# Expert stage of a two-block model: a finished expert group leaves its accumulators ahead of two weight splits, its scatter stands one expert later, and the branch is taken ahead of the first gather

## The chip, the cores and the metric

The kernel runs on one core of one Trainium2 chip. The metric is the time of one execution on the device in microseconds, the median of several executions. The engines are TensorE (PE; its weight loads are shown as PEld), VectorE (DVE), ScalarE (ACT), GpSimd (POOL) and SyncE (SP, which here only issues weight loads).

## The reference, cut to what matters

The program is a first block (two feed-forward parts and a mixer) and a second block of two layers. Each layer of the second block mixes tokens and then runs a mixture of experts over 256 tokens of width 1024. The change touches the expert part alone:

```python
N_EXPERTS = 16; N_GROUPS = 4; EXPERTS_PER_GROUP = 4; TOP_K = 2; D_EXPERT = 256
scores = jax.nn.sigmoid((t @ router_w).astype(jnp.float32))
biased = scores + router_bias
grp_score = jnp.sum(lax.top_k(biased.reshape(T, 4, 4), TOP_K)[0], -1)
sel_group = jnp.argmax(grp_score, -1)             # one group of four experts per token
_, top_idx = lax.top_k(jnp.where(in_group, biased, -jnp.inf), TOP_K)
gates = ...                                       # two experts inside that group, normalised
h = jnp.einsum('td,edf->tef', t, w_gate_up)
a = jax.nn.silu(h[..., :D_EXPERT]) * h[..., D_EXPERT:] * gates[..., None]
y = jnp.einsum('tef,efd->td', a, w_down)
```

A token uses experts of one group only. So the four experts of a group work on the tokens of that group, at most 128 of them here, and their outputs can be added up before they go back to token order.

## The kernel before, in words

**Weights.** All weights are 32-bit and are used as a sum of two 16-bit parts. They come in units of 128 x 2048 values (1 MiB) through a ring of six slots (RING, line 33). SP loads a unit into `raw` (load, line 493) once the low part of the unit six before has been made. ScalarE makes the high part `whi` (hi_part, line 393; it waits for the load and for TensorE to have used the unit six before). VectorE makes the low part `wlo` (lo_part, line 402; it waits for the high part). These two instructions are a split. TensorE multiplies in three products, high x high, high x low and low x high (split_mm, line 621). An expert has three units, two of gate/up weights and one of down weights.

**The order of the work is written out by hand**, one list of instructions per engine, joined by semaphores. Each engine works through its own list in order. `emit(n)` on ScalarE (line 1547) and on VectorE (line 2070) stands for the next n splits of the ring.

**Ahead of the experts.** TensorE computes router logits and counts, for every token, its rank within its group (lines 1095 to 1099). VectorE's `ranks` (line 2034) copies the ranks and writes the largest group size into `rr[:, 18]`, with semaphore `rank_out`. VectorE's `places` (line 2040) then builds the selection matrices `p16`. TensorE's `gather(0)` (line 1101) multiplies the tokens with the matrix of group 0, so that its tokens stand in 128 slots. Now it is called ahead of the branch (lines 1112 to 1115). ScalarE and VectorE copy the result out as `ugh` and `ugl`. Each of the three engines then reads the largest group size into a register and branches (line 1267 on TensorE): over 128 tokens the dense way, otherwise the sparse way. The sparse way runs here, in both layers.

**Sparse way, TensorE (line 1242).** For each expert c of 16: `slots_in_half(c)` is the gate/up matmul of the group's slots, 96 matmuls of 128 columns in two halves, one for each weight unit. After experts 0 to 2 the gather of the next group follows. From c = 2 on `slots_down(c - 2)` follows, the down-projection, 12 matmuls of 512 columns. The down-projections of the four experts of a group add up in two PSUM banks, 6 and 7, the group's accumulators. `slots_down(4g)` opens them anew, so it waits until the earlier group has left them (`ys_lo`, line 1196). `scatter(g)` (line 1228, matmuls on line 1234) multiplies the group's 16-bit output with the transposed selection matrix, 8 matmuls of 512 columns, and adds it to the tokens' PSUM banks 0 to 3. It waits for `ys_lo` too. It stands after `slots_in_half` of c = 6, 10 and 14 for groups 0 to 2, and at the end for group 3.

**Sparse way, ScalarE (line 1590) and VectorE (line 2113).** For each expert ScalarE does the SiLU (line 1596), one split, the high part of the activations (line 1612) and two more splits. VectorE does the product (lines 2120 and 2126), one split, the low part of the activations (line 2131) and two more splits. At c = 5, 9 and 13 `group_out` follows these, for groups 0, 1 and 2: ScalarE copies the accumulators as `ysh` (line 1587, two instructions; it waits for the last down-projection of the group and, for the same buffer, for the scatter of two groups before). VectorE makes the rest `ysl` (line 2110, two instructions; `ys_lo`).

Of the kernel before, what the change touches and what calls it, by code (L numbers as in the profile page):

```python
# [37 lines left out]
EXPERTS = 16  # L38
# [121 lines left out]
def build(nc, a, out):  # L160
    small_d, b1_d, b2_d = a["const_small"], a["const_block1"], a["const_block2"]
    with ExitStack() as ctx:
# [457 lines left out]
        def _(pe):  # L620
# [325 lines left out]
            for l in range(LAYERS):  # L946
# [154 lines left out]
                def gather(g):  # L1101

                    for half in range(2):
                        for i, v in enumerate((xh, xl)):
                            for k in range(4 * half, 4 * half + 4):
                                o = ps[:, 2 * i + half, (k % 4) * P:(k % 4 + 1) * P]
                                for t in range(TT):
                                    last = pe.matmul(o, v[:, t, k * P:(k + 1) * P], p16[:, t, g * P:(g + 1) * P],  # L1108
                                                     start=t == 0, stop=t == 1)
                            last.then_inc(ga_mm[l], 1)  # L1110

                pe.wait_ge(xt_out, 4 * l + 4)
                pe.wait_ge(p_made0, 2 * l + 2)
                pe.wait_ge(rank_out, l + 1)
                gather(0)

                def gates():

# [13 lines left out]

                def dense():

                    pe.wait_ge(gates_made, l + 1)
                    gates()
                    pe.wait_ge(ga_hi[l], 2)
                    pe.wait_ge(ga_lo[l], 2)
                    residual()

                    def expert_down(c):
                        u = at_down(l, c)
                        pe.wait_ge(e_lo_made, EXPERTS * l + c + 1)
                        pe.wait_ge(lo_made, u.count(1))
                        hi, lo = ([v[:, c % 3, f * T:(f + 1) * T] for f in range(2)] for v in (d_hi, d_lo))
                        done = c == EXPERTS - 1
                        down(u, hi, lo, stop=done, done=True if done else None)

                    for c in range(EXPERTS):
                        if c >= 2:  # L1150
                            pe.wait_ge(e_m, EXPERTS * l + c - 1)
                        for half in range(2):
                            u = at_in(l, c) + half
                            pe.wait_ge(lo_made, u.count(1))
                            for kk in range(4):
                                k = 4 * half + kk
                                for col in range(4):
                                    w = slice(kk * HALF + col * P, kk * HALF + (col + 1) * P)
                                    last = split_mm(ps[:, 4 + 2 * (c % 2) + col // 2, (col % 2) * T:(col % 2 + 1) * T],
                                                    whi[:, u.slot, w], wlo[:, u.slot, w], uhi[:, k, :], ulo[:, k, :],  # L1160
                                                    k == 0 and col % 2 == 0, k == KT - 1)
                            last.then_inc(used, 1)
                        if c >= 2:
                            expert_down(c - 2)
                    expert_down(EXPERTS - 2)
                    expert_down(EXPERTS - 1)
                    pe.matmul(ps[0:32, 4, 0:1], zeros16[0:1, 0:32], zeros16[0:1, 0:1], start=True, stop=True,
                              skip_group_check=True).then_inc(used, 1)
# [71 lines left out]
                        last.then_inc(sc_mm2[l], 1)  # L1240

                def sparse():
                    for c in range(EXPERTS):
                        if c == 1:
                            pe.wait_ge(pT_out[l], 1)
                        slots_in_half(c)
                        if c == 0:
                            slot_setup()
                        if c < 3:
                            pe.wait_ge(ga_hi[l], 2 * c + 2)  # L1250
                            pe.wait_ge(ga_lo[l], 2 * c + 2)
                            gather(c + 1)
                        if c == 1:
                            pe.wait_ge(gbs_out[l], 4)
                        if c == 3:
                            pe.wait_ge(ga_hi[l], 8)
                            pe.wait_ge(ga_lo[l], 8)
                            residual()
                        if c in (6, 10, 14):
                            scatter(c // 4 - 1)  # L1260
                        if c >= 2:
                            slots_down(c - 2)
                    slots_down(EXPERTS - 2)
                    slots_down(EXPERTS - 1)
                    scatter(3)

                count = pe.value_load(rr[0:1, 18, 0:1].bitcast(I32))
                with pe.If(count > P):
                    dense()
# [7 lines left out]
        def _(act):  # L1277
# [130 lines left out]
            for i in range(10):  # L1408
# [14 lines left out]
                else:  # L1423
                    c = 256 * (i - 7)
# [27 lines left out]
            for l in range(LAYERS):  # L1452
# [137 lines left out]
                def sparse():  # L1590
                    emit(1)
                    for c in range(EXPERTS):
                        act.wait_ge(used, (at_in(l, c) + 1).count(1))
                        if c:
                            act.wait_ge(e_m, EXPERTS * l + c)
                        act.activation(e_act, ps[:, 4 + c % 2, 0:T], ACT.Silu, scale=1.0 / S).then_inc(e_silu, 1)
                        if c == 0:
                            act.wait_ge(pT_mm[l], 1)
                            act.activation(pT16.rearrange("p g n -> p (g n)"), ps[:, 5, :].bitcast(F16), ACT.Copy,
                                           scale=S / SX).then_inc(pT_out[l], 1)  # L1600
                            for g in range(4):
                                act.wait_ge(gbs_mm[l], g + 1)
                                act.activation(gbs[:, 4 * g:4 * g + 4, :],
                                               ps[:, 6 + g % 2, :].rearrange("p (k n) -> p k n", k=4),
                                               ACT.Copy).then_inc(gbs_out[l], 1)
                        if c < 3:
                            gather(c + 1)
                        emit(1)
                        act.wait_ge(e_made, EXPERTS * l + c + 1)
                        if c >= 3:  # L1610
                            act.wait_ge(used, at_down(l, c - 3).count(1))
                        act.activation(e_hi[:, c % 3, :], e_h, ACT.Copy).then_inc(e_hi_made, 1)
                        emit(2 if c < EXPERTS - 1 else 1)
                        if c in (5, 9, 13):
                            group_out(c // 4 - 1)
                    act.activation(flag[:, 5:6], zero8[:, 0:1], ACT.Sqrt)
                    group_out(3)

# [15 lines left out]
        def _(dve):  # L1634
# [286 lines left out]
            for l in range(LAYERS):  # L1921
# [191 lines left out]
                def sparse():  # L2113
                    emit(1)
                    for c in range(EXPERTS):
                        dve.wait_ge(e_silu, EXPERTS * l + c + 1)
                        if c:
                            dve.wait_ge(e_hi_made, EXPERTS * l + c)
                            dve.wait_ge(e_lo_made, EXPERTS * l + c)
                        dve.scalar_tensor_tensor(out=e_h, in0=ps[:, 4 + c % 2, T:2 * T], scalar=SX / S, in1=e_act,  # L2120
                                                 op0=ALU.mult, op1=ALU.mult).then_inc(e_m, 1)
                        if c == 0:
                            dve.wait_ge(gbs_out[l], 4)
                        dve.wait_ge(e_m, EXPERTS * l + c + 1)
                        hv = e_h.rearrange("p (k n) -> p k n", k=2)
                        dve.tensor_tensor(hv, hv, gbs[:, c, :].unsqueeze(1).to_broadcast([P, 2, P]), ALU.mult)                            .then_inc(e_made, 1)
                        if c < 3:
                            gather(c + 1)
                        emit(1)
                        dve.wait_ge(e_hi_made, EXPERTS * l + c + 1)  # L2130
                        dve.tensor_tensor(e_lo[:, c % 3, :], e_h, e_hi[:, c % 3, :], ALU.subtract).then_inc(e_lo_made, 1)
                        emit(2 if c < EXPERTS - 1 else 1)
                        if c in (5, 9, 13):
                            group_out(c // 4 - 1)
                    group_out(3)

                dve.wait_ge(gates_made, l + 1)
# [41 lines left out]
```

## Time and profile before

| | |
|---|---|
| median of 3 executions | 1338.1 us (1336.7 to 1341.34) |
| profiled execution, its own time | 1342.71 us |
| its span | 1340.9 us |
| mean granted clock of TensorE | 0.929 |
| TensorE matmuls busy | 1169.8 us, 87% |
| VectorE busy | 930.3 us, 69% |
| ScalarE busy | 667.9 us, 50% |
| expert stage of layer 0 | about 820 to 979 us of the span |
| expert stage of layer 1 | about 1167 to 1327 us of the span |

The span begins and ends with the profiled instructions; the execution's own time holds a little more. Lines such as L625 are helpers that many stages call, so their totals over the whole span say little about the expert stage. It has to be read in windows. The granted clock is the share of full speed that the chip gives to TensorE.

### The profile page before, as it was taken

Reading aid. Unit: us, or ns where it says so; the run is one execution under the profiler, and the core shown is the slowest. Engines: PE = TensorE matmul, PEld = TensorE weight load, DVE = VectorE, ACT = ScalarE, POOL = GpSimd, SP = SyncE. Lnnn points to the kernel's source line nnn. Section 1 sums busy time; section 2 is a strip of 40 time slices with the busy share of each in tenths; the row PEclk is TensorE's granted clock in tenths of the full one; section 3 lists DMA queues with packets and bytes.
Section 4 is the critical chain, followed back from the end, with each engine's and each line's share of the span. In section 5 each row is a group of like instructions: output and inputs, shape, how many; then the busy total and the mean of one; then the engine's idle time right before and its main releaser. Section 6 shows DMA issues by size and latency. Waiting matters only on the chain.

```text
span 1340.9 us, 24182 instructions
## 1 busy us (share of the span) xinstructions
PE 1169.8 (87%) x10316; PEld 900.0 (67%) x10316; DVE 930.3 (69%) x1145; ACT 667.9 (50%) x819; POOL 58.2 (4%) x75
## 2 busy tenths in 40 slices
PE   0499999799898899999897888999979978799995
PEld 0387777487786487776685548877668755697773
DVE  6689999465557555554548756998864775689985
ACT  1254433243345444442446546776653554577772
POOL 1001110150000000000100000000000000000000
PEclk9999999789798899999999797999989979699998
DMA  6999998423057365555544031999935303079970
GB/s 231 352 356 374 372 376 300 146 86 119 0 179 276 112 242 188 188 189 169 187 134 130 1 126 65 331 372 337 331 99 174 112 32 125 4 283 381 338 257 32
DMA packets 155451, 271.73 MB, mean 203 GB/s; under 512 B 9205, under 2 KB 95402, under 8 KB 155226
## 3 DMA queue, kind: packets, MB, share of 16 engines
q1 hardware_dynamic: 145946, 228.50, 49.4%
q0 software_dynamic: 6144, 32.41, 6.1%
q10 hardware_dynamic: 3264, 9.44, 2.1%
q8 instruction: 72, 1.18, 0.3%
q14 instruction: 25, 0.20, 0.0%
HBM read 269.28 MB, written 1.05 MB: 202 GB/s over the span
## 4 chain that ended last, share of the span: by engine, by line
PE 56%; DVE 28%; ACT 7%; issue 7%; DMA 1%; SPq 0%; DVEq 0%; ACTq 0%
PE ps L625 43%; DVE wlo L408 12%; DVE area L1728 6%; ACT whi L400 2%; PE ps L1234 1%; ACT area L1360 1%; DVE stat L1784 1%; DVE area L1778 1%; PE ps L826 1%; PE ps L815 1%; PE ps L872 1%; DMA area<-in_w_ada_dram 1%; PE ps L1108 1%; PE ps L705 1%; DVE hreg L1711 1%
## 5 line engine op out<-in xcount | busy, mean ns | idle before, releaser
L408 DVE SCALAR_TENSOR_TENSOR wlo<-raw,whi 128x2048 f16<-128x2048 f32 (+4 forms) x228 | 488.0, 2172 | 113.7 <-ACT whi L400 112.2
L400 ACT ACTIVATE whi<-raw 128x2048 f16<-128x2048 f32 (+4 forms) x228 | 403.3, 1805 | 34.8 <-PE ps L625 21.7
L625 PE MATMUL ps<-uhi,whi 128*128 128x256 f16 (+1 forms) x1200 | 326.1, 274 | 8.3 <-DVE ulo L1693 4.1
L625 PE MATMUL ps<-ulo,whi 128*128 128x256 f16 (+1 forms) x1200 | 326.0, 274 | 0.0
L625 PE MATMUL ps<-uhi,wlo 128*128 128x256 f16 (+1 forms) x1200 | 325.8, 273 | 0.0
L625 PE MATMUL ps<-whi,hreg 128*128 128x512 f16 x736 | 233.1, 387 | 5.4 <-DVE hreg L1716 5.4
L625 PE MATMUL ps<-area,whi 128*128 128x128 f16 (+2 forms) x2168 | 200.5, 225 | 8.6 <-issue 4.4
L625 PE MATMUL ps<-area,wlo 128*128 128x128 f16 (+2 forms) x1084 | 194.0, 225 | 0.0
L625 PEld LDWEIGHTS ps<-area,whi 128*128 128x128 f16 (+2 forms) x2168 | 175.1, 100 | 19.2 <-issue 8.2
L625 PE MATMUL ps<-wlo,hreg 128*128 128x512 f16 x368 | 142.5, 387 | 0.0
L625 PEld LDWEIGHTS ps<-uhi,whi 128*128 128x128 f16 x1200 | 119.3, 99 | 31.0 <-issue 8.8
L625 PEld LDWEIGHTS ps<-whi,hreg 128*128 128x128 f16 x736 | 73.5, 100 | 92.5 <-issue 8.3
L625 PEld LDWEIGHTS ps<-ulo,whi 128*128 128x128 f16 x1200 | 119.2, 99 | 17.4 <-issue 2.0
L625 PEld LDWEIGHTS ps<-uhi,wlo 128*128 128x128 f16 x1200 | 119.4, 99 | 13.9
L625 PEld LDWEIGHTS ps<-area,wlo 128*128 128x128 f16 (+2 forms) x1084 | 109.0, 101 | 0.0
L1728 DVE SCALAR_TENSOR_TENSOR area<-area,cond 128x768 f32 (+1 forms) x96 | 97.7, 1017 | 9.7 <-DMA area<-in_w_ada_dram 3.2
L1333 ACT ACTIVATE hreg<-ps 128x512 f32<-128x512 f32 x22 | 13.0, 593 | 103.9 <-PE ps L625 103.9
L625 PEld LDWEIGHTS ps<-wlo,hreg 128*128 128x128 f16 x368 | 36.7, 100 | 40.4 <-issue 4.2
L1335 ACT ACTIVATE hreg<-hreg 128x512 f16<-128x512 f32 x22 | 13.9, 630 | 88.3 <-DVE hreg L1711 88.3
L1711 DVE SCALAR_TENSOR_TENSOR hreg<-ps,hreg 128x512 f32<-128x512 f32 x22 | 15.1, 688 | 60.7 <-ACT hreg L1333 60.7
L1458 ACT ACTIVATE area<-ps 128x512 f32<-128x512 f32 (+4 forms) x32 | 17.4, 550 | 71.1 <-PE ps L625 60.5
L1360 ACT ACTIVATE area<-area,stat 128x128 f32<-128x128 f32 (+3 forms) x56 | 27.6, 493 | 39.0 <-DVE stat L1791 39.0
(300 smaller groups left out, 1383.5 us busy)
## 6 DMA issues: line engine op xcount, KB each, us to landing
raw<-in_exp_w_gate_up_dram SPq DMA_DIRECT2D x64, 1024.0 KB, 7.4
raw<-in_w_ffn_in_dram SPq DMA_DIRECT2D x44, 1024.0 KB, 7.4
raw<-in_w_in_dram SPq DMA_DIRECT2D x34, 1024.0 KB, 6.0
raw<-in_exp_w_down_dram SPq DMA_DIRECT2D x32, 1024.0 KB, 8.0
area<-in_w_ada_dram POOLq DMA_DIRECT2D x36, 768.0 KB, 7.7
raw<-in_w_ffn_out_dram SPq DMA_DIRECT2D x22, 1024.0 KB, 7.3
raw<-in_w_out_dram SPq DMA_DIRECT2D x12, 1024.0 KB, 5.8
area<-in_w_ada_dram ACTq DMA_DIRECT2D x12, 768.0 KB, 6.0
```

What stands on the lines that cost most here:

```text
L400: act.activation(whi[:, u.slot, 0:n], raw[:, u.slot, 0:n], ACT.Copy, scale=SW).then_inc(hi_made, 1)
L408: dve.scalar_tensor_tensor(out=wlo[:, u.slot, 0:n], in0=raw[:, u.slot, 0:n], scalar=SW, in1=whi[:, u.slot, 0:n], op0=ALU.mult, op1=ALU.sub ...
L625: last = pe.matmul(o, st, mv, start=start and i == 0, stop=stop and i == 2, skip_group_check=True)
L705: last = pe.transpose(ps[:, 4 + k // 2, (k % 2) * T + t * P:(k % 2) * T + (t + 1) * P], xn[:, t, k * P:(k + 1) * P], ident)
L815: pe.matmul(ps[:, n % 3, 128:384], q[:, 128:256], k, start=True, stop=True).then_inc(sc_mm, 1)
L826: last = pe.transpose(ps[:, 3 + n % 3, c * P:(c + 1) * P], src[:, c * P:(c + 1) * P], ident)
L872: last = pe.matmul(ps[:, 4, 8 * j + c:8 * j + c + 1], acc[:, m * D + c * P:m * D + (c + 1) * P], ones[:, 0:1], start=True, stop=True)
L1335: act.activation(hhi[:, par, :], h_f32, ACT.Copy).then_inc(h_hi, 1)
L1360: last = act.activation(s_, s_, ACT.Exp, bias=st[:, 2 + t:3 + t], accum_out=st[:, 4 + t:5 + t])
L1458: act.activation(dst, src, func, scale=1.0 / S).then_inc(proj_out, 1)
L1711: dve.scalar_tensor_tensor(out=h_f32, in0=ps[:, 5 + 2 * par, :], scalar=SX / S, in1=s_act, op0=ALU.mult, op1=ALU.mult).then_inc(h_made, 1)
L1728: dve.scalar_tensor_tensor(out=v, in0=aring[:, k // 2, k % 2, :], scalar=cond[:, k:k + 1], in1=v, op0=ALU.mult, op1=ALU.add).then_inc(ada_ ...
```

## The change

Three edits, in both layers. On ScalarE and VectorE `group_out` of groups 0 to 2 stands ahead of the expert's last two splits instead of behind them. On TensorE the scatter of groups 0 to 2 stands after the gate/up matmuls of experts 7, 11 and 15 instead of 6, 10 and 14. And TensorE's wait for the largest group size, the register load and the branch stand ahead of the first gather, which is now the first thing in either way.

```diff
--- before.py
+++ after.py
@@ tensor
-                pe.wait_ge(xt_out, 4 * l + 4)
-                pe.wait_ge(p_made0, 2 * l + 2)
-                pe.wait_ge(rank_out, l + 1)
-                gather(0)
+                def first_gather():
+
+                    pe.wait_ge(xt_out, 4 * l + 4)
+                    pe.wait_ge(p_made0, 2 * l + 2)
+                    gather(0)
...
                 def dense():
 
+                    first_gather()
                     pe.wait_ge(gates_made, l + 1)
...
                 def sparse():
+                    first_gather()
                     for c in range(EXPERTS):
...
-                        if c in (6, 10, 14):
+                        if c in (7, 11, 15):
                             scatter(c // 4 - 1)
                         if c >= 2:
                             slots_down(c - 2)
...
+                pe.wait_ge(rank_out, l + 1)
                 count = pe.value_load(rr[0:1, 18, 0:1].bitcast(I32))
                 with pe.If(count > P):
                     dense()
@@ scalar
                         act.activation(e_hi[:, c % 3, :], e_h, ACT.Copy).then_inc(e_hi_made, 1)
-                        emit(2 if c < EXPERTS - 1 else 1)
                         if c in (5, 9, 13):
                             group_out(c // 4 - 1)
+                        emit(2 if c < EXPERTS - 1 else 1)
@@ vector
                         dve.tensor_tensor(e_lo[:, c % 3, :], e_h, e_hi[:, c % 3, :], ALU.subtract).then_inc(e_lo_made, 1)
-                        emit(2 if c < EXPERTS - 1 else 1)
                         if c in (5, 9, 13):
                             group_out(c // 4 - 1)
+                        emit(2 if c < EXPERTS - 1 else 1)
```

## Rows read from the trace of the kernel before

**Rows 1.** The page, busy us, share of the span, instructions, TensorE.
```profile
PE 1169.8 (87%) x10316; PEld 900.0 (67%) x10316; DVE 930.3 (69%) x1145; ACT 667.9 (50%) x819; POOL 58.2 (4%) x75
```

**Rows 2.** Chain of waits, 880 to 925 us: start, us, what.
```profile
884.10 0.69 DVE area L2110
...
884.85 1.90 PE ps L1234 x8
```

**Rows 3.** Timeline of TensorE, experts 5 and 6: start, us, instruction [idle before].
```profile
869.37 0.28 PE L625 MATMUL ps<-area,whi 128*128 128x128 f16 x2
...
874.73 0.38 PE L625 MATMUL ps<-whi,hreg 128*128 128x512 f16 x1
...
877.32 0.28 PE L625 MATMUL ps<-area,whi 128*128 128x128 f16 x2
...
884.85 1.90 PE L1234 MATMUL ps<-area 128*128 128x512 f16 x8 [2.00 <-DVE area L2110]
...
886.58 0.38 PE L625 MATMUL ps<-whi,hreg 128*128 128x512 f16 x1
...
889.17 0.28 PE L625 MATMUL ps<-area,whi 128*128 128x128 f16 x2
```

**Rows 4.** Timeline of TensorE, second stop of layer 0, last of layer 1.
```profile
913.02 0.28 PE L625 MATMUL ps<-area,whi 128*128 128x128 f16 x2
...
920.54 3.06 PE L1234 MATMUL ps<-area 128*128 128x512 f16 x8 [1.99 <-DVE area L2110]
...
926.55 0.28 PE L625 MATMUL ps<-area,whi 128*128 128x128 f16 x2
...
1297.97 0.28 PE L625 MATMUL ps<-area,whi 128*128 128x128 f16 x2
...
1311.49 0.28 PE L625 MATMUL ps<-area,whi 128*128 128x128 f16 x2
```

**Rows 5.** Windows: stretch, length, busy by engine, granted clock, DMA share, GB/s.
```profile
820.00:824.00 4.00, 3.78 (x36) 3.81 (x37) 3.59 (x14) 1.11 (x1) 0.00 (x0) 0.50 0.02 4
...
876.00:884.00 8.00, 6.84 (x103) 5.93 (x101) 7.97 (x7) 7.22 (x8) 0.00 (x0) 1.00 1.04 393
...
916.00:924.00 8.00, 6.01 (x56) 3.71 (x54) 7.96 (x8) 6.02 (x7) 0.00 (x0) 0.82 1.04 398
```

**Rows 6.** Timeline of VectorE, step of expert 5 and accumulators of group 0.
```profile
876.37 0.41 DVE L2120 SCALAR_TENSOR_TENSOR hreg<-ps,hreg 128x256 f32<-128x256 f32 x1
...
879.70 4.49 DVE L408 SCALAR_TENSOR_TENSOR wlo<-raw,whi 128x2048 f16<-128x2048 f32 x2
884.10 1.28 DVE L2110 SCALAR_TENSOR_TENSOR area<-ps,area 128x512 f16<-128x512 f32 x2
```

**Rows 7.** Timeline of ScalarE, the same stretch.
```profile
877.60 3.69 ACT L400 ACTIVATE whi<-raw 128x2048 f16<-128x2048 f32 x2
881.20 1.06 ACT L1587 ACTIVATE area<-ps 128x512 f16<-128x512 f32 x2
```

**Rows 8.** Timeline of SP, landing of that load, ScalarE's split of it.
```profile
884.21 0.37 SPq L498 DMA_DIRECT2D raw<-in_exp_w_down_dram  x1
...
DMA to landing us min/median/max: 9.9/9.9/9.9
...
898.92 1.90 ACT L400 ACTIVATE whi<-raw 128x2048 f16<-128x2048 f32 x1
```

**Rows 9.** Timeline around the branch, VectorE's count, then TensorE in both layers.
```profile
813.80 0.15 DVE L2038 CAST area<-area 128x1 int32<-128x1 f32 x1
...
814.70 1.55 PE L1108 MATMUL ps<-area 128*128 128x128 f16 x18 [1.42 <-DVE area L2042]
...
820.22 0.37 PE L625 MATMUL ps<-area,whi 128*128 128x128 f16 x2 [2.48 <-issue]
...
828.10 0.61 PE L1211 MATMUL ps<-diag,area 128*128 128x128 f16 x8
...
1167.14 0.37 PE L625 MATMUL ps<-area,whi 128*128 128x128 f16 x2 [1.91 <-issue]
...
1173.98 0.22 PE L1211 MATMUL ps<-diag,area 128*128 128x128 f16 x1
```

## The prediction

> **What bounds the kernel now.** I read the page first: TensorE is busy for 87% of the span, so in most stages it sets the pace and what counts is where it stands still [rows 1]. Then the chain of waits through the expert stage of layer 0. It goes back from a scatter (line 1234) to VectorE's accumulator step (line 2110) [rows 2]. So I took the timeline of TensorE alone. From the start of expert 0 to the end of the last down-projection, its stops of more than half a microsecond all lie ahead of scatter(0), scatter(1) and scatter(2). One expert costs 5.36 us for its gate/up matmuls (869.37 to 874.73) and 2.59 us for a down-projection (874.73 to 877.32), 7.95 us together [rows 3]. Gate/up of expert 6 starts at 877.32 and is through at 882.68 by that count, but scatter(0) starts at 884.85 with 2.00 us of idle time put down to line 2110. The scatter itself takes 1.73 us at full clock (884.85 to 886.58) and the down-projection after it 2.59.
>
> The cost of a stop is best read from the start of one gate/up to the start of the next. First stop: 877.32 to 889.17 is 11.85 us, where 5.36 + 1.73 + 2.59 = 9.68 would do. 2.17 us are lost [rows 3]. The other five lose more: 913.02 to 926.55 is 13.53 and 1297.97 to 1311.49 is 13.52, so 3.85 each [rows 4]. The extra 1.68 us is the clock: the eight matmuls of scatter(1) span 3.06 us against 1.90 in scatter(0), and the granted clock of the 8 us around the stop is 0.82 against 1.00 for the eight around the first. Between stops the clock is 1.00 [rows 4, 5]. Total in the six stops: 2.17 + 5 x 3.85 = 21.4 us.
>
> **Accumulators ahead of two splits.** Per group two ScalarE copies and two VectorE subtractions move ahead of two splits on each engine; nothing is added and the move holds no DMA. On VectorE, expert 5 begins at 876.37, its low half is done where the two splits begin, at 879.70, and the accumulator step follows them at 884.10, 1.28 us long by the row and 1.20 us in pitch [rows 6]. ScalarE's copies stand at 881.20 behind two splits from 877.60, 1.06 us [rows 7]. In the new order ScalarE copies from about 877.6 to 878.7. What it waits for, the end of down-projection 3, is there at 877.32 [rows 3]. VectorE then works from 879.70 to about 880.9 instead of 884.1 to 885.3, 4.4 us earlier. TensorE wants the result at 882.68, where down-projection 4 re-uses those banks. It is ready with some 1.7 us to spare, so the wait doesn't reappear there. Here ScalarE comes to them 2.9 us after gate/up 5 ends, and the down-projection takes 2.59; where ScalarE is less behind it may wait some tenths, which the 1.7 us hold.
>
> **What is queued behind.** The two splits that now follow are 1.2 us later on VectorE. TensorE needs the earlier of them (second half of expert 7) at 885.27 + 2.68 = 887.95; it is done at 883.1. The other (down weights of expert 5) is done at 885.3 and read at 892.4. Next expert's step starts at 885.3 as before. SP loads a ring slot only after the split of the unit six before, so two loads per group go out 1.2 us later. The tightest one was issued at 884.21, took 9.9 us to land (894.1), and ScalarE split it at 898.92, 4.8 us later [rows 8]. With TensorE's stop gone ScalarE comes 2.2 us sooner, and with the load 1.2 us later about 1.4 us is left. If that is used up ScalarE stalls, but TensorE reads this unit only some 8 us after the split, so the first microseconds cost nothing.
>
> **Scatter one expert later.** Eight matmuls per group stand behind gate/up 7, 11, 15 instead of 6, 10, 14; their input is then 8 us old. The same number of matmuls, at full clock 1.73 us, no cost. The buffer of group g is next written by group g+2, eight experts on, so no new wait. At 15 it also gives expert 15's low half 1.7 us more cover ahead of its down-projection.
>
> **Is VectorE next?** It needs 7.73 us per expert (876.37 to 884.10) against TensorE's 7.95, and per group 4 x 7.73 + 1.2 = 32.1 against 4 x 7.95 + 1.73 = 33.5 [rows 3, 6]. It stays 1.4 us per group inside. Followed expert by expert with these durations, the distance between the two only grows in VectorE's favour after group 0, and the last group's tail is as before. So all 21.4 us should go. Bounds: 0 if every wait comes back at the down-projection, 21.4 if none does. I take 21.4, since the spare time of 1.7 us is from rows.
>
> **The branch ahead of the first gather.** Now the gather starts at 814.70, behind VectorE's first selection matrices, and expert 0 at 820.22 with 2.48 us idle put down to issue; in layer 1 it is 1.91 us [rows 9]. That is value_load and branch. The count is out at 813.95 (813.80 + 0.15). Behind a wait on it the branch would let the gather start at 813.95 + 1.9 to 2.5 = 815.9 to 816.5, some 1.5 us later than now, and expert 0 follows the gather at once: its inputs for the first half were copied a microsecond before. Net -1.0 us in layer 0, -0.4 in layer 1. Then the clock. Expert 0 ran at half (0.50 from 820 to 824) and took 7.88 us up to 828.10; in layer 1 it took 6.84, where 5.36 would do: 2.5 and 1.5 us lost [rows 5, 9]. Gather and expert 0 become one unbroken run of 7.2 us at full clock, and what was a second slow start between them falls away; the first remains. I count half of the 4.0 us. Layer 0 and 1 together: -1.4 - 2.0 = -3.4, taken as 3. Bounds: -6 if the whole slow start goes, +2 if the branch takes 2.5 us longer in its new place, with the gather's own instructions behind it. VectorE's gate chain shifts later by some 1.5 us with the gather, and is still through before expert 0 ends; slot_setup does not wait long.
> The row shows only that the branch costs 1.91 to 2.48 us behind a gather. The Trainium skill (Runtime: NRT & Kernel Launch, "Instruction fetch mechanics") says that prefetch is sequential and that a taken branch out of the window stops the sequencer for a fetch. By that rule the move hides none of the stall except the 0.75 us in which TensorE waits for VectorE anyway, and both layers would give 1.5 us of idle time and what the clock gives beside it; no row here shows a fetch.
>
> **Sum.** Against the profiled execution's own 1342.7 us (span 1340.9, 1.8 around it): -21.4 - 3 = 1318.3. That execution is 4.6 us over the median of 1338.1; I take the difference, 24.4, off the median: **1314 us**, -1.8%.
>
> **Rivals.**
> A. The wait comes back ahead of down-projection 4g, one expert earlier than the scatter it left. VectorE would have to be over 1.7 us later against TensorE than the rows have it, for which the saturated VectorE of experts 4 to 6 speaks (busy 7.97 of 8 us [rows 5]), and its 1.4 us of slack per group against. With 1 us of waiting and the clock's 1.68 in all six: 21.4 - 16 = 5.4 saved, and 3 from the branch: 1330.
> B. Weights become the bound. A group's 12 loads of 1.05 MB in 33.5 us are 375 GB/s. The DMA share is already 1.04 with 393 GB/s in the stretch before the first stop and loads took up to 9.9 us there [rows 5, 8]. For it: landing times rise while VectorE asks for three loads per 7.73 us. Against: 393 is above 375, and no engine waits for a weight load in this stage now. If the rate stayed at what the stage moves now per group (12.6 MB in 37.4 us, 337 GB/s), 3.85 us of each of 4 groups would be lost again, less some 8 us that the ring is ahead: about 7.4 per layer, 15 in all, time 1329.
> The Trainium skill (DMA: Bandwidth & Descriptors, "Where 436 GB/s comes from") gives about 358 GB/s per core for loads from HBM. The 393 of the trace is over that. As an estimate by the page, a group would take 35.1 us in place of 33.5; the 6.4 us in four groups are within the ring's 8, or cost up to 3 us in both layers, 1317.
> C. The move is one for one: accumulators can't leave earlier, since ScalarE's copies wait for down-projection 4g+3, and TensorE stops as long at the new place. Against: that projection ends at 877.32, ScalarE started the copies 3.9 us later [rows 3, 7]. Time 1336 to 1338.
> D. Slower. VectorE falls behind at the down-projection as in A, but by 3 us: each stop then costs 3 + 1.68 = 4.7, six of them 28 against the 21.4 removed: 1338.1 + 6.7 - 3 = 1342. It decides from the point where VectorE is 5.6 us later against TensorE than now (1.7 spare + 3.85 paid today), which a lost 0.6 us per expert would bring about by the third group.
>
> **Chances.** Forecast 0.78, A 0.07, B 0.07, C 0.05, D 0.03. Nine tenths lie between 1309 (branch bound of -6, executions a little under the median) and 1331; with a tenth to each side left out I give 1309 to 1328. Faster by over 0.3% (4 us, about what a measurement of this kernel tells from no change): 0.92, within 0.3%: 0.05, slower: 0.03.
>
> **What would show it.** Right: no idle time on TensorE ahead of any scatter but the last of a layer; 9.68 us from gate/up 7 to gate/up 8; granted clock 1.00 from expert 1 to 15; line 2110 about 4.4 us earlier against expert 5's step; gather at 816 and expert 0 directly behind it. Wrong: idle time put down to line 2110 ahead of a down-projection (A, C, D); ScalarE's line 400 waiting for a DMA of expert weights (B); a gather later than 817.

## The result and the profile after

| | before | changed |
|---|---|---|
| median | 1339.13 us (1336.7 to 1341.34, 4 runs) | 1319.53 us (1317.37 to 1321.82, 4 runs) |
| profiled execution, own time | 1342.71 us | 1319.91 us |
| its span | 1340.9 us | 1318.1 us |
| mean granted clock | 0.929 | 0.939 |

The ratio is 0.9852, with a 95% interval of 0.9831 to 0.9874: 19.6 us faster by the medians, 22.8 us by the two profiled executions. Beside it on another chip the changed kernel came to 0.9819 (0.98 to 0.9839), 23.1 us (experiment 5). The forecast was 24.4 us less.

**The stops are gone.** TensorE's timeline of the changed kernel around the first scatter, lines that answer to [rows 3]: start, us, instruction, and in brackets idle time where there is any.

```profile
877.26 0.28 PE L625 MATMUL ps<-area,whi 128*128 128x128 f16 x2
...
882.62 0.38 PE L625 MATMUL ps<-whi,hreg 128*128 128x512 f16 x1
...
885.21 0.28 PE L625 MATMUL ps<-area,whi 128*128 128x128 f16 x2
...
890.57 1.89 PE L1236 MATMUL ps<-area 128*128 128x512 f16 x8
...
892.29 0.38 PE L625 MATMUL ps<-whi,hreg 128*128 128x512 f16 x1
...
894.88 0.28 PE L625 MATMUL ps<-area,whi 128*128 128x128 f16 x2
```

Gate/up 6 ends and down-projection 4 starts at 882.62 with no bracket behind it. From gate/up 7 (885.21) to gate/up 8 (894.88) it is 9.67 us, 9.68 by the forecast's count. The other five places read the same: from scatter to scatter it is 33.52 or 33.53 us in both layers. In the chain of waits of the changed kernel the groups follow each other as matmuls alone: start, us, what.

```profile
858.93 31.80 PE ps L625 x432
890.73 1.73 PE ps L1236 x8
892.46 31.80 PE ps L625 x432
924.26 1.73 PE ps L1236 x8
925.98 31.80 PE ps L625 x432
957.78 1.73 PE ps L1236 x8
```

31.80 + 1.73 = 33.53 us per group, the count of the forecast, where the kernel before took 35.7 or 37.4.

**Why TensorE finds the result ready.** VectorE's timeline of the changed kernel, the step of expert 5; it answers to [rows 6]. The accumulators leave at 879.63, directly behind the low half of expert 5's activations, and the splits follow from 880.83. TensorE wants the first bank at 882.62. Both halves of the result are there 1.7 to 1.8 us earlier; the forecast had 1.7. The true spare time is longer. Each half has a wait of its own in the down-projection (line 1196 of the kernel before), the first half is done 0.68 us after the start, at 880.31, and only this half is wanted at 882.62. That is 2.3 us.

```profile
879.29 0.42 DVE L2135 TENSOR_TENSOR hreg<-hreg 128x256 f16<-128x256 f32 x1
879.63 1.28 DVE L2114 SCALAR_TENSOR_TENSOR area<-ps,area 128x512 f16<-128x512 f32 x2
880.83 4.48 DVE L408 SCALAR_TENSOR_TENSOR wlo<-raw,whi 128x2048 f16<-128x2048 f32 x2
```

**Clock and weights.** A window of 100 us in the changed kernel's expert stage, columns as in [rows 5], and all waits that the profile lists from 850 to 960 us: who waited for whom, total us, times, longest.

```profile
850.00:950.00 100.00, 100.00 (x1355) 81.97 (x1353) 97.33 (x80) 75.77 (x66) 0.00 (x0) 1.00 1.03 379
```

```profile
ACT hreg L1600 <- PE ps L625: 15.5, 12, 2.6
ACT hreg L1616 <- DVE hreg L2130: 10.4, 9, 2.8
DVE wlo L408 <- ACT whi L400: 1.8, 2, 0.9
```

TensorE is busy for all of 100 us, the clock is full, VectorE is at 97%, the weights arrive at 379 GB/s, and nobody waits for a load.

**The branch.** Here the profile differs from the forecast. TensorE's timeline of the changed kernel, the lines that answer to [rows 9]:

```profile
818.97 3.25 PE L1108 MATMUL ps<-area 128*128 128x128 f16 x29 [4.81 <-issue]
822.34 0.42 PE L625 MATMUL ps<-area,whi 128*128 128x128 f16 x2
828.04 0.61 PE L1213 MATMUL ps<-diag,area 128*128 128x128 f16 x8
...
1153.50 3.89 PE L1108 MATMUL ps<-area 128*128 128x128 f16 x32 [4.82 <-issue]
1157.19 0.42 PE L625 MATMUL ps<-area,whi 128*128 128x128 f16 x2
1162.72 0.61 PE L1213 MATMUL ps<-diag,area 128*128 128x128 f16 x8
```

The idle time ahead of expert 0 is gone, but 4.81 us stand ahead of the gather where 1.42 stood. The view of the branch's own line gives the cause: the compare-and-branch in TensorE's queue, of the kernel before (line 1268) and of the changed one (line 1272). The three numbers are the shortest, median and longest in ns.

```profile
L1268 PEldq COMPARE_BRANCH  x2: 3466/3670/3873, 816.2 to 1163.5; - x2
```

```profile
L1272 PEldq COMPARE_BRANCH  x2: 3358/3454/3551, 815.4 to 1149.8; - x2
```

It lasts about as long in both places. Before, it began at 816.2, while the array still worked on the gather up to 817.7: the queue had taken in all of the gather, and 1.5 us of the branch were hidden under it (1.7 in layer 1). Ahead of the gather the array has nothing left to do.

ScalarE and VectorE take the same way in the same kernel, over their own dense ways, and their branches cost next to nothing. The same view for the kernel before, lines 1621 and 2139:

```profile
L1621 ACTq COMPARE_BRANCH  x2: 45/50/54, 817.5 to 1164.8; - x2
...
L2139 DVEq COMPARE_BRANCH  x2: 63/65/67, 823.4 to 1170.7; - x2
```

So taking the branch is not enough to make it dear. TensorE's dense way has 96 gate/up matmuls for each of 16 experts, and those of the other two have only a few instructions and three splits for each.

### The profile page after: what moved, and what is told of

Same layout as the page of the kernel before. It is cut to its first block, busy times and chain, and to the rows that moved or that the text cites. A ratio compares the mean times of both kernels' runs of the same rounds, so it can differ in the third digit from the quotient of the medians.

```text
span 1318.1 us, 24182 instructions
## 1 busy us (share of the span) xinstructions
PE 1157.3 (88%) x10316; PEld 894.2 (68%) x10316; DVE 929.4 (71%) x1145; ACT 667.6 (51%) x819; POOL 58.2 (4%) x75
## 4 chain that ended last, share of the span: by engine, by line
PE 66%; DVE 21%; ACT 6%; issue 5%; DMA 1%; SPq 0%; DVEq 0%; ACTq 0%
PE ps L625 53%; DVE wlo L408 6%; DVE area L1732 6%; PE ps L1108 1%; ACT area L1364 1%; ACT whi L400 1%; DVE stat L1788 1%; DVE area L1782 1%; PE ps L1236 1%; PE ps L729 1%; PE ps L826 1%; PE ps L815 1%; PE ps L872 1%; PE ps L705 1%; DMA area<-in_w_ada_dram 1%
## 5 line engine op out<-in xcount | busy, mean ns | idle before, releaser
L625 PE MATMUL ps<-whi,hreg 128*128 128x512 f16 x736 | 229.6, 382 | 5.4 <-DVE hreg L1720 5.4
L625 PE MATMUL ps<-area,whi 128*128 128x128 f16 (+2 forms) x2168 | 196.7, 223 | 4.2 <-DVE area L1967 4.2
L625 PE MATMUL ps<-area,wlo 128*128 128x128 f16 (+2 forms) x1084 | 190.3, 223 | 0.0
```

The lines of the kernel that those rows point to most:

```text
L625: last = pe.matmul(o, st, mv, start=start and i == 0, stop=stop and i == 2, skip_group_check=True)
```

## The experiments

Experiments 1 to 4 ran on one chip, 5 to 8 on a second and 9 and 10 on a third, each time beside the kernel before; times and ratios are against it. Only the lines that an edit changes are printed, against the changed kernel unless said otherwise; three dots stand for code left out.

### 1. Groups only: the branch stays behind the first gather

```diff
-                def first_gather():
-
-                    pe.wait_ge(xt_out, 4 * l + 4)
-                    pe.wait_ge(p_made0, 2 * l + 2)
-                    gather(0)
+                pe.wait_ge(xt_out, 4 * l + 4)
+                pe.wait_ge(p_made0, 2 * l + 2)
+                pe.wait_ge(rank_out, l + 1)
+                gather(0)
...              (first_gather() goes out of both ways)
-                pe.wait_ge(rank_out, l + 1)
                 count = pe.value_load(rr[0:1, 18, 0:1].bitcast(I32))
```

> Accumulators ahead of the splits and scatter one expert later; the branch stays behind the first gather. Theory 1 (the gain is the six stops, 2.17 + 5 x 3.85 = 21.4 us, and the moved branch is worth next to nothing: its idle time grew from 2.48 + 1.42 to 4.81 us in layer 0 while the slow start got shorter): 21 us under the kernel before, within 1 to 2 us of the changed kernel, idle ahead of expert 0 again about 2.5 and 1.9 us. Rival 1 (the branch carries the forecast's 3 us): 18 us under before. Rival 2 (the moved branch costs, since its compare-and-branch of 3.4 us stands alone ahead of the gather): this kernel is 1 to 3 us faster than the changed one.

1317.77 us against 1342.22: 0.9825 (0.9801 to 0.9849), 24.4 us faster. No stop ahead of scatters 0 to 2 in either layer, idle time ahead of expert 0 back at 2.26 and 2.02 us. From the first router matmul to the end of expert 0 its profile has 19.84 and 18.22 us, 38.06 together, where the changed kernel has 38.18. So the forecast's 24.4 us are reached without the moved branch; against the changed kernel's 0.9852 and 0.9819 no difference can be told.

### 2. Branch only

```diff
-                        if c in (7, 11, 15):
+                        if c in (6, 10, 14):
...              (ScalarE and VectorE)
-                        if c in (5, 9, 13):
-                            group_out(c // 4 - 1)
                         emit(2 if c < EXPERTS - 1 else 1)
+                        if c in (5, 9, 13):
+                            group_out(c // 4 - 1)
```

Against the kernel before, only the branch has moved.

> Only the branch stands ahead of the first gather; accumulators and scatter as before. Theory 1: within 2 us of the kernel before, idle time ahead of the gather 4.8 us in both layers, none ahead of expert 0, and the six stops stay at 2.0 us of idle each. Rival 1: 3 us faster. Rival 2: 1 to 3 us slower.

1335.12 us against 1342.22: 0.995 (0.9935 to 0.9964), 7.1 us faster, more than any theory had. Idle time ahead of the gather is 4.79 us in both layers and none stands ahead of expert 0. Most of the gain is not at the branch. From the first router matmul to the end of expert 0 this kernel takes 18.99 and 19.45 us, against 19.97 and 20.01 before: 1.5 us. Most of the rest seems to stand in the stops, which this profile has all six, each with 2.0 us idle. TensorE's timeline of this kernel, second and third stop of layer 0:

```profile
917.18 1.90 PE L1236 MATMUL ps<-area 128*128 128x512 f16 x8 [1.99 <-DVE area L2114]
...
952.88 3.56 PE L1236 MATMUL ps<-area 128*128 128x512 f16 x8 [2.00 <-DVE area L2114]
```

The same 2.0 us of idle time once leave the scatter at 1.90 us and once at 3.56. Measured from gate/up to gate/up, a stop costs 2.17 us or 3.84, hardly anything between: here four times the small price and twice the large, 16.4 us, in the profile before once and five times, 21.4 us. This goes beyond one profile: the mean granted clock is 0.936 to 0.942 in the 12 executions of this kernel, and 0.929 to 0.935 in the 23 of the kernel before beside them. On the other two chips the kernel before reached 0.937 and 0.939, though. The reading is that with the moved branch fewer of the stops lower the clock, and that this gain falls away once there are no stops. It fits the runs but is not shown: one profile of each kernel was kept, and these two also differ by 2.4 us ahead of the router and by 1.4 us, the other way, between the layers, where the kernels are the same. What decides whether a stop of 2 us lowers the clock stays open.

### 3. Accumulators only: the scatter stays at 6, 10, 14

```diff
-                        if c in (7, 11, 15):
+                        if c in (6, 10, 14):
                             scatter(c // 4 - 1)
```

The branch stays behind the gather as in experiment 1, so against the kernel before only `group_out` has moved.

> Only the accumulators leave ahead of the two splits; the scatter stays at experts 6, 10 and 14, the branch as before. Theory 1 (the stop was the late low half, and that is 1.7 us early at the old scatter too): no stop ahead of a scatter, same time as with the later scatter within 1 us, 21 us under before. Rival 3 (both moves are needed, since the scatter takes the result as soon as it is there): stops of 0.3 us or more ahead of the scatters and 3 us or more slower than with both.

1317.31 us, 0.9828 (0.9802 to 0.9854), 24.9 us faster: the same as with the later scatter. Its scatter(0), at the old place, has no bracket:

```profile
879.07 1.89 PE L1234 MATMUL ps<-area 128*128 128x512 f16 x8
```

The whole gain that can be measured is in the accumulators' place. The second edit adds nothing to it.

### 4. Scatter only

The edit is against the kernel before.

```diff
-                        if c in (6, 10, 14):
+                        if c in (7, 11, 15):
                             scatter(c // 4 - 1)
```

> Only the scatter stands one expert later; the accumulators leave behind the splits as before. Theory 1 (down-projection 4g re-uses the banks, so it waits for the same low half): the stop moves one for one from the scatter to down-projection 4, 8, 12, about 2.0 us of idle each, clock at half behind it in most; time of the kernel before within 2 us. Rival 4 (the later scatter is what removes the stop): 15 to 21 us faster.

1338.54 us, 0.9979 (0.9965 to 0.9993), 3.7 us faster, where at most 2 were expected. TensorE's timeline of this kernel shows the stop of group 0 at down-projection 4 instead of the scatter:

```profile
883.70 0.38 PE L625 MATMUL ps<-whi,hreg 128*128 128x512 f16 x1 [2.10 <-DVE area L2110]
```

All six are there, moved one for one, twice at 2.25 us and four times at 3.92, 20.2 us together. This is rival C of the prediction, true of the scatter's move alone. The 3.7 us are not explained; the stops' prices in the two profiles differ by 1.2.

### 5. The changed kernel again, beside three other branches

> The changed kernel once more, on one chip beside the next three. Theory 1: 19 to 23 us under before. It is the base of the comparison with the other branch orders.

1316.83 us against 1339.97: 0.9819 (0.98 to 0.9839), 23.1 us faster. The next three ran beside it.

### 6. The sparse way directly behind the compare, branch behind the gather

The gather stands as in experiment 1. On top of that:

```diff
-                with pe.If(count > P):
-                    dense()
+                with pe.If(count <= P):
+                    sparse()
                 with pe.Else():
-                    sparse()
+                    dense()
```

> Groups as in the change, the branch behind the first gather as before, and on TensorE the condition turned round, so that the way that is taken stands directly behind the compare and the dense way behind it. The trace has compare-and-branch at 3.4 to 3.9 us. Theory 5 (the sequencer waits for instructions from a far place; The Trainium skill, Runtime: NRT & Kernel Launch, 'Instruction fetch mechanics', says a taken branch out of the window has to fetch): compare under 0.5 us, no idle time ahead of expert 0, 2.3 and 2.0 us of idle less and less of the slow start, 4 to 8 us faster than with the branch as before. A jump of 3.5 us over the dense way then stands behind the last scatter of layer 0, half hidden by the 2.8 us in which TensorE waits there. Rival 5 (the compare itself costs 3.5 us whichever way it goes): no difference.

1311.8 us, 0.9781 (0.9761 to 0.9801): 5.0 us under the changed kernel, from which it differs in two edits. From experiment 1 it differs in this one alone; that ran on another chip, and 0.9781 against 0.9825 is 5.9 us. No idle time between gather and expert 0. Theory 5 holds, and rival 5 does not. Behind the last scatter of layer 0 TensorE stands for 3.54 us instead of 2.83, so the jump over the dense way shows there with 0.7 us. TensorE's timeline of this kernel, at that place:

```profile
969.66 1.83 PE L715 MATMUL ps<-small,xn 128*128 128x128 f32 x8 [3.54 <-DVE xn L1676]
```

### 7. The same with the branch ahead of the gather

The turned condition of experiment 6 on the changed kernel; nothing else differs.

> The changed kernel with the condition turned round on TensorE. Theory 5: idle time ahead of the gather back from 4.8 to about 1.4 us, none ahead of expert 0, the same time as the last one within 1 us or up to 1 us faster. Rival 5: 4.8 us stay, same time as the changed kernel.

1310.56 us, 0.9775 (0.9755 to 0.9795): 29.4 us under the kernel before and 6.3 under the changed kernel, the cleanest comparison, with one edit on one chip. From experiment 6 it can't be told. The line of the branch, the whole kernel and then layer 0's compare alone:

```profile
L1272 PEldq COMPARE_BRANCH  x4: 80/1956/4420, 810.4 to 1294.0; - x4
...
L1272 PEldq COMPARE_BRANCH  x1: 80/80/80, 810.4 to 810.4; - x1
```

And TensorE's timeline, at the gather, where VectorE's selection matrices end the idle time again, and behind the last scatter of layer 0, where the idle time is 3.44 us against the changed kernel's 2.83:

```profile
810.61 3.14 PE L1108 MATMUL ps<-area 128*128 128x128 f16 x32 [1.52 <-DVE area L2046]
...
819.38 0.61 PE L1213 MATMUL ps<-diag,area 128*128 128x128 f16 x8
...
964.51 1.82 PE L715 MATMUL ps<-small,xn 128*128 128x128 f32 x8 [3.44 <-DVE xn L1680]
```

The same instruction takes 80 ns when it falls through; in the kernels with the dense way first it is taken to a place behind that way and takes 3.3 to 3.9 us. The two long ones of the four are now jumps at the end of the layers (4.42 and 3.83 us). The Trainium skill (Runtime: NRT & Kernel Launch, "Instruction fetch mechanics") says that prefetch is sequential and that a taken branch out of the window has to fetch first. These runs agree, with 0.08 against 3.5 us on TensorE and 0.05 to 0.07 us for the taken branches of ScalarE and VectorE over their much shorter dense ways. No run has a near target on TensorE.

### 8. No branch on TensorE

```diff
-                count = pe.value_load(rr[0:1, 18, 0:1].bitcast(I32))
-                with pe.If(count > P):
-                    dense()
-                with pe.Else():
-                    sparse()
+                sparse()
```

It leaves out TensorE's dense way, which these inputs don't take.

> Groups as in the change; TensorE has no register load, no compare and no dense way (it always goes the sparse way, which is what these inputs ask for); ScalarE and VectorE branch as before. It measures all that TensorE's branch costs: Theory 5 and Rival 5 both expect no idle time ahead of expert 0 and 4 to 8 us under the kernel with groups only; if the kernel with the sparse way first is within 1 us of it, nothing of the branch is left to gain.

1310.21 us, 0.9777 (0.9752 to 0.9801). Its interval is 3.3 us to each side, and it can't be told from experiments 6 and 7. Of what the branch costs on TensorE, turning the condition round gets back all that can be measured. In the profile TensorE stands for 2.83 us behind the last scatter of layer 0 here, so 0.6 to 0.7 us of the jump are left in those two.

### 9. Accumulators between the two splits

```diff
                         if c in (5, 9, 13):
+                            emit(1)
                             group_out(c // 4 - 1)
-                        emit(2 if c < EXPERTS - 1 else 1)
+                            emit(1)
+                        else:
+                            emit(2 if c < EXPERTS - 1 else 1)
```

> The changed kernel with the accumulators leaving between the two splits, one ahead and one behind, on both engines. It tests the 1.7 us of spare time at down-projection 4g: VectorE's low half comes one split (2.2 us) later, its first part at about 882.5 and its second at 883.1 in group 0, against a need at 882.7 and 884.0. Theory 1: stops of 0 to 0.5 us ahead of down-projections 4, 8, 12 that don't lower the clock, time within 2 us of the changed kernel. Rival A of the prediction (VectorE is so late that the wait comes back): stops of 1.5 us or more and 5 us or more over the changed kernel.

1316.83 us against 1339.88: 0.9833 (0.9805 to 0.9862), 23.1 us faster, as much as the changed kernel in experiment 5. No bracket ahead of down-projections 4, 8 and 12 or scatters 0 to 2; from scatter(0) at 887.86 to scatter(1) at 921.43 it is 33.57 us, 0.04 more than in the changed kernel. VectorE's accumulators and TensorE's down-projection 4 in this kernel:

```profile
879.09 1.28 DVE L2117 SCALAR_TENSOR_TENSOR area<-ps,area 128x512 f16<-128x512 f32 x2
...
879.92 0.38 PE L625 MATMUL ps<-whi,hreg 128*128 128x512 f16 x1
```

The accumulators are 2.2 us later, more than the 1.7 us of the prediction, and still nothing stops: the first half is out at 879.77, 0.15 us ahead of the down-projection. This fits a spare time of 2.3 us. One split behind the accumulators is enough, and rival A's wait does not arise even with nearly all of the spare time used up.

### 10. ScalarE's copies behind the splits, VectorE's part ahead

```diff
 # ScalarE only
+                        emit(2 if c < EXPERTS - 1 else 1)
                         if c in (5, 9, 13):
                             group_out(c // 4 - 1)
-                        emit(2 if c < EXPERTS - 1 else 1)
```

> The changed kernel with ScalarE's copies behind its two splits as before, VectorE's part ahead of its splits. VectorE then stands at its wait for the copies (from 879.6 to about 881.9 in group 0) with both splits queued behind it. Theory 1: the low half is there at 883.2, TensorE stops 0.1 to 0.3 us at down-projection 4, VectorE loses 2 us per group, of which its slack per group takes 1.4; stops grow a little in groups 1 and 2, time 0 to 4 us over the changed kernel. Rival 6 (ScalarE's order doesn't matter): no difference and no idle time on VectorE.

1321.96 us, 0.9868 (0.9841 to 0.9895), 5.1 us over experiment 9 beside it, a little more than expected. VectorE now stands for the copies with its splits queued behind them. TensorE does not stop in group 0, and stops for 0.5 us in groups 1 and 2. In layer 0 it stops once more ahead of the last down-projection, for expert 15's activations, which no theory had. VectorE's and TensorE's timeline of this kernel, in layer 0:

```profile
879.07 1.29 DVE L2114 SCALAR_TENSOR_TENSOR area<-ps,area 128x512 f16<-128x512 f32 x2 [2.03 <-ACT area L1591]
...
914.16 0.38 PE L625 MATMUL ps<-whi,hreg 128*128 128x512 f16 x1 [0.52 <-DVE area L2114]
...
948.40 0.38 PE L625 MATMUL ps<-whi,hreg 128*128 128x512 f16 x1 [0.56 <-DVE area L2114]
...
964.37 0.39 PE L625 MATMUL ps<-whi,hreg 128*128 128x512 f16 x1 [0.95 <-DVE hreg L2135]
```

From scatter to scatter the four stops of 0.5 us cost 0.7 us each, and the scatter behind them spans 1.89 us: stops this short don't lower the clock here. The last one costs 1.1 us. That is 3.9 of the 5.1 us. So VectorE's part alone brings most of the gain, 17.9 of some 23 us, and ScalarE's part the rest.

## Why the prediction was right, and where it was off

- **Where the time stood.** Right. Six stops, 21.4 us, all gone. Experiment 1 has this, with the later scatter, at 24.4 us (20.3 to 26.7 by its interval), and 3 and 4 show that the accumulators' place does it.
- **The wait does not come back at down-projection 4g.** Right, and with more to spare than was worked out: 1.7 us count from the end of both halves, but at 882.6 only the first is wanted, so it is 2.3. Experiment 9 used up a split of 2.2 us of it and lost nothing. Rivals A and D did not occur.
- **Scatter later at no cost.** Right; at no gain either (3 against 1).
- **VectorE stays inside, the supply holds.** Right. A group takes 33.53 us as counted. Rival B does not occur: 379 GB/s over 100 us is above the 375 asked for, where the kernel before moved 357 in the same window. The Trainium skill's 358 GB/s for loads from HBM (DMA: Bandwidth & Descriptors, "Where 436 GB/s comes from") is passed here; the measurement decides.
- **The two later loads.** The load that had 9.9 us in [rows 8] was issued at 885.3 in the changed kernel and landed 8.5 us later. No engine waited for one.
- **The branch.** The direction of its total was right and its terms were not. The forecast had the gather start 1.5 us later than before and 1.4 us less idle time over both layers. Measured from the count (814.70 + 0.15) the gather starts 4.1 us later instead of 1.9 to 2.5. In layer 0 the idle time grew from 1.42 + 2.48 to 4.81 us, in layer 1 from 1.42 + 1.91 to 4.82, 2.4 us in all. The step that failed is "that is value_load and branch": the 1.91 to 2.48 us of idle time were taken for the whole cost of the branch, and they were only what stuck out from under the gather. The branch's own line, 3.47 to 3.87 us in the kernel before, was there to be read; the register load ahead of it is 0.3 to 0.5 us more. The estimate that the prediction set beside the fetch rule, 1.5 us of idle time gained in both layers, fails on the same step: it took it that before none of the stall was hidden, and 1.5 to 1.7 us of it were in each layer. The clock gave more than the half that was counted: expert 0 took 5.70 and 5.53 us against 7.88 and 6.84, 3.5 us where 2.0 were taken. The stage from the first router matmul to the end of expert 0 went from 19.97 and 20.01 to 19.01 and 19.17 us: 1.8 us gained, of 3.4 worked out, of which 3 went into the sum. Even of these 1.8, 1.1 stand in layer 1 between the first router matmul and the last rank matmul, ahead of the branch in both kernels (6.27 against 5.13 us); experiments 1, 3 and 4, with the branch in its old place, have 5.23 to 5.27 there. And experiment 1 takes no longer over the whole stage than the changed kernel. A gain by the moved branch, beside the accumulators, is not shown.
- **The sum.** 21.4 + 1.8 = 23.2, and the profiled executions differ by 22.8: 23.7 from the first router matmul of layer 0 on, and 0.9 the other way ahead of it, where the kernels are the same (that matmul stands between 804 and 809 us in all profiles). The medians of the first measurement differ by 19.6 (16.9 to 22.6 by the interval), those in experiment 5 by 23.1. The time came out 5.5 us over the forecast. 1.0 of this is the kernel before, whose median is 1339.13 here and was taken at 1338.1, and 1.2 is the branch, 1.8 in place of 3. The other 3.6 no row explains: 23.2 lies just above the interval of the first measurement and inside that of experiment 5 (21.6 to 26.8). One cause was not tested: the 21.4 us were read from one execution, which took longer than the other three known by then, and in which five of six stops were dear. Experiments 2 and 4 have two and four dear ones, and with fewer of them there is less to save.
- The prediction named a gather later than 817 as a sign that its branch step was wrong. It came at 818.97. The signs for the accumulators were all met: no idle time ahead of scatters 0 to 2, 9.67 us from gate/up to gate/up, a granted clock of 1.00 from expert 1 on, and the accumulators 4.4 us earlier against expert 5's step.

## What to carry to other kernels

When an engine that bounds the time stands still at a point, look in the queue of the engine that it waits for at what stands ahead of the awaited instruction, and let the awaited work go first if the work behind it has slack. Price such a stop from start to start of the repeating work, clock included, and expect it to be worth more or less when its place shifts. Put the way that is taken directly behind the compare, and don't take idle time behind a branch for its cost: look at the branch's own line in the queue.

## What the runs showed of the hardware

- A compare-and-branch on TensorE took 0.08 us when it fell through and 3.3 to 3.9 us when it was taken over the dense way; 1.5 to 1.7 us of this were hidden while the array worked through matmuls issued ahead of it. ScalarE's and VectorE's, taken over their short dense ways, took 0.05 to 0.07 us.
- The same stop of 2.0 us cost either 2.17 or 3.85 us. Stops of 0.5 us cost 0.7 (experiment 10).
- With 3.4 us more idle time ahead of the gather, and the stops as before, the mean granted clock was 0.936 to 0.942 against 0.929 to 0.935 on the same chip, and the time 7.1 us less, of which 1.5 stood at the moved place (experiment 2). Why is not shown.
- Sixteen DMA engines delivered 379 GB/s over 100 us to one core.
